# The odd mixer's heads: which engine makes the low parts of the weight units

## The reference, cut to what matters

```
proj = h @ w_in                               # q, k, v, o (16 heads x 128 each), gates ig, fg
q, k = silu(conv4(q)), silu(conv4(k))         # depthwise, causal, 4 taps
# per head, over the 512 tokens, with stabilised exponential gates:
sw  = (q k^T) * weights(gates)                # causal
num = sw @ v ; den = sum(sw)
h   = num / max(|den|, exp(-m)) ; h = rmsnorm(h) * head_norm
y   = sigmoid(o) * h ; x = x + y @ w_out
```

## Time and profile before

| | |
|---|---|
| time of the profiled execution | 4507.37 us |
| its span, first to last instruction | 4505.9 us |
| mean granted TensorE clock | 0.979 of full |
| TensorE busy with matmuls | 4281.0 us, 95% |
| VectorE busy | 2660.6 us, 59% |
| ScalarE busy | 2114.7 us, 47% |
| GpSimd busy | 1237.0 us, 27% |
| low parts on VectorE (L163) | 585 instructions |
| low parts on GpSimd (L170) | 109 instructions |
| the 15 bodies of the odd mixer | 2236.53 to 2710.15 us |

### The profile page before, as it was taken

How to read it: one execution, slowest core, us unless ns; L and a number is a source line. 1 busy time by engine, 2 the same in 40 slices (tenths; PEclk the granted TensorE clock), 3 DMA queues, 4 the chain that set the end, 5 groups by cost and what they waited for, 6 DMA issues and landing times. The chain is left out here.

```text
span 4505.9 us, 61663 instructions
## 1 busy us (share of the span) xinstructions
PE 4281.0 (95%) x19295; PEld 3459.1 (77%) x19295; DVE 2660.6 (59%) x5626; ACT 2114.7 (47%) x4073; POOL 1237.0 (27%) x1571
## 2 busy tenths in 40 slices
PE   7999899999999999999798988999999999999997
PEld 5665687888888888887577776787888888888885
DVE  3546589777764444444566663687877754444444
ACT  2755343677763333333345452433787743333324
POOL 0210245777750000000100000345888720000000
PEclk9999999999999999999899999999999999999998
DMA  2111233555566656542122222334555575656531
GB/s 100 62 47 40 82 116 125 208 180 200 179 256 211 206 172 209 182 159 83 50 75 77 74 77 70 112 117 163 186 203 182 200 261 192 209 170 207 187 121 56
DMA packets 178192, 653.90 MB, mean 145 GB/s; under 512 B 17200, under 2 KB 17328, under 8 KB 172928
## 3 DMA queue, kind: packets, MB, share of 16 engines
q1 hardware_dynamic: 100944, 371.41, 25.2%
q0 software_dynamic: 40240, 213.69, 13.4%
q10 hardware_dynamic: 36864, 67.13, 4.0%
HBM read 507.42 MB, written 144.74 MB: 145 GB/s over the span
## 5 line engine op out<-in xcount | busy, mean ns | idle before, releaser
L184 PE MATMUL ps<-h_hi,w_hi 128*128 128x512 f32 x4296 | 1698.6, 395 | 153.2 <-PEq L280 52.0
L184 PE MATMUL ps<-h_hi,w_lo 128*128 128x512 f32 x4296 | 1683.8, 392 | 0.0
L184 PE MATMUL ps<-h_lo,w_hi 128*128 128x512 f32 x4296 | 1683.7, 392 | 0.0
L163 DVE TENSOR_TENSOR w_lo<-w_raw,w_hi 128x1024 fp32r<-128x1024 f32 x585 | 718.5, 1228 | 1047.7 <-ACT w_hi L157 1042.8
L157 ACT ACTIVATE w_hi<-w_raw 128x1024 fp32r<-128x1024 f32 x694 | 735.8, 1060 | 903.7 <-PE ps L184 730.3
L184 PEld LDWEIGHTS ps<-h_hi,w_hi 128*128 128x128 f32 x4296 | 813.1, 189 | 334.8 <-issue 91.4
L184 PEld LDWEIGHTS ps<-h_hi,w_lo 128*128 128x128 f32 x4296 | 812.5, 189 | 173.4
L184 PEld LDWEIGHTS ps<-h_lo,w_hi 128*128 128x128 f32 x4296 | 814.0, 189 | 160.9 <-issue 0.2
L1481 POOL TENSOR_SCALAR second_hot<-iota,token_keys 128x128 fp32r<-128x128 f32 x1024 | 721.7, 718 | 0.0
L1519 ACT ACTIVATE first_scaled<-first_hot,token_keys 128x128 fp32r<-128x128 f32 x1792 | 542.3, 390 | 0.5 <-DVE first_scaled L1451 0.4
L170 POOL TENSOR_TENSOR w_lo<-w_raw,w_hi 128x1024 fp32r<-128x1024 f32 x109 | 282.9, 2597 | 716.9 <-ACT w_hi L157 716.9
(11 more groups left out here) (308 smaller groups left out, 3516.0 us busy)
## 6 DMA issues: line engine op xcount, KB each, us to landing
w_raw<-in_u SPq DMA_DIRECT2D x256, 512.0 KB, 3.6
w_raw<-in_v SPq DMA_DIRECT2D x256, 512.0 KB, 3.6
gates<-gate_group POOLq DMA_DIRECT2D x36, 2048.0 KB, 8.0
acts<-gelu ACTq DMA_DIRECT2D x256, 256.0 KB, 2.2
gate_block<-gates POOLq DMA_DIRECT2D x32, 2048.0 KB, 18.2
gelu_block<-acts POOLq DMA_DIRECT2D x30, 2048.0 KB, 11.9
w_raw<-in_od_in SPq DMA_DIRECT2D x65, 512.0 KB, 3.5
w_raw<-in_ev_in SPq DMA_DIRECT2D x33, 512.0 KB, 3.5
```

The source lines that it names most:

```text
L163: self.nc.vector.tensor_tensor(self.wl[:, slot % SPL, :], self.raw[:, slot, :], self.wh[:, slot % SPL, :].bitcast(F32), ALU.subtract).then ...
L184: ins = self.nc.tensor.matmul(out, a[:, s, w], b[:, k, :], start=first and j == 0 and m == 0, stop=last and j == n - 1 and m == 2)
```

## The change

Five edits, all in `OddMixer`:

1. GpSimd makes its fifth low part (unit 0 of head 1) behind `rsel` and the transfer of the rows to memory, and no longer ahead of them.
2. For each head n = 1 to 15 it makes, behind the issue of the row's transfer, the low parts of units 1, 2, 3 and of the next unit 0: 60 instructions.
3. VectorE no longer makes these 60. The rest of its order is the same.
4. In head 0, ScalarE makes the high part of unit 2 of the head ahead of the silu of k instead of behind it.
5. VectorE's wait for GpSimd's fifth low part ahead of the bodies is gone; behind the bodies it waits for GpSimd's last one before it makes the output units' low parts.

```diff
-        for n in range(5):
+        for n in range(4):
             p.split_lo_pool(pool, self.u0 + n + 1, (self.u0 + n + 1) % RAW)
         pool.wait_ge(self.cleared.sem, self.cleared.at(1))
         pool.wait_ge(self.gin.sem, self.gin.at(3))
         g.tensor_scalar(self.rsel[:, :], self.negG[:, :], p.ident[0:HEADS, 0:1], None, ALU.mult
                         ).then_inc(self.se.sem, 1)
         pool.dma_start(self.held, self.negG[:, :]).then_inc(self.kept.sem, 16)
+        p.split_lo_pool(pool, self.u0 + 5, (self.u0 + 5) % RAW)
         pool.wait_ge(self.kept.sem, self.kept.at(16))
         for n in range(1, HEADS):
             if n > 1:
                 pool.wait_ge(self.ag.sem, self.ag.at(4 * n))
             pool.dma_start(self.row[:, :], self.held[n:n + 1, :].to_broadcast([P, T])).then_inc(self.bc.sem, 16)
+            for j in range(4):
+                p.split_lo_pool(pool, self.h0 + 4 * n + j + 1, (self.h0 + j + 1) % RAW)
@@ scalar
         a.activation(r["ln"], r["ab"], ACT.Ln).then_inc(self.gact.sem, 1)
+        split(0, 1)
         silu(0, 0)
-        split(0, 1)
         split(0, 2)
@@ vector
-        dve.wait_ge(p.sig("w_lo_ready").sem, h0 + 5)
         def body(n, half, i):
             link.enter(i, self.STEP)
-            lo(n, 0)
             conv(n, 0)
-            lo(n, 1)
             normed(n)
             conv(n, 1)
-            lo(n, 2)
             taken_v(n)
             gate(n)
-            lo(n, 3)
@@
+        dve.wait_ge(p.sig("w_lo_ready").sem, o0 + 1)
         ahead(0)
```

More of the change, by code:

```diff
@@ L2027, in vector @@
         negG, cols, qk, tmp = self.negG, self.cols, self.qk, self.tmp
-        def lo(n, j):
-            p.split_lo(dve, n * 4 + h0 + j + 1, (h0 + j + 1) % RAW)
         def conv(n, j):
```

## The result

Four runs of the changed kernel took 4458.38 us (median; 4457.17 to 4461.97) against 4508.48 (4507.08 to 4509.66): ratio 0.989, 95% interval 0.9873 to 0.9907. The forecast was 4464, the range 4455 to 4482. The profiled execution took 4457.17, its span is 4455.6 us, 50.3 shorter than before.

What follows compares the result with a forecast made beforehand. TensorE, busy 95%, was taken to bound the kernel, waiting 3.3 us a body for VectorE's low part of unit 3 behind conv of q. 4507.4 - 28.5 (bodies) - 3.9 (head 0) - 11.3 (clock) = 4463.7 us; range 4455 to 4482.

Steps and rivals of the forecast that it cites:

- The steady body: Each of the 15 mixer bodies falls from 30.7 to 28.8 us, 28.5 us in all, between 18 and 33.
- D: Rival: GpSimd's low parts, length L, stretch; TensorE starts unit 3 at 10.0 + 2L; slower, 4532 us; chance 0.04.
- the signs by which I would have called the prediction wrong: Bodies above 29.5 us at full clock, TensorE waiting for VectorE's last copy ahead of `output`, or low clocks staying.
- VectorE's loop: VectorE's work per body, including being held by GpSimd: 28.7 us, about as long as TensorE's.
- TensorE's chain through unit 2: In a body: unit 0's product, conv of k, silu, high part, GpSimd's low part, unit 2's product; 28.6 us.
- the worked-out 28.6: TensorE's loop per body: unit 3 starts at 14.9 instead of 17.03, so 30.7 becomes 28.6 us.
- What the engines do to each other: VectorE and GpSimd instructions reading SBUF alone exclude each other for their whole length, the later waiting: the lock.
- Rival B: VectorE's loop decides, through meetings with GpSimd at the masks and late conv of k: body 29.5, 4474 us; chance 0.18.
- Head 0: `rsel` no longer waits behind GpSimd's fifth low part, starting at 2218.9 instead of 2222.84: 3.9 us gained.
- The clock: Of 13.0 us lost to 1.2 GHz stretches in the bodies, 11.3 return, between 0 and 13; 1.7 may stay.
- Rival A: The clock doesn't come back in the bodies, low stretches stay as many: 4475 us; chance 0.12.
- C: Rival: the bodies get no relief, TensorE's wait returning at unit 2; only head 0 pays: 4503 us; chance 0.02.

Runs made afterwards that it cites:

- order: The kernel before with one line moved: VectorE makes unit 3's low part ahead of conv of q, nothing goes to GpSimd; 4445.12 us, ratio 0.9859.
- stretch: The changed kernel with a GpSimd memset of about 1.8 us between high and low part of units 2 and 3 in each body; 4510.87 us, ratio 1.0009.
- bodies: The changed kernel with head 0 as before (edits 1 and 4 taken back); 4462.79 us, ratio 0.9899.
- head0: The kernel before with edits 1 and 4 alone, all low parts of the bodies staying on VectorE; 4504.14 us, ratio 0.9993.
- order_head0: The kernel before with unit 3's low part moved ahead of conv of q on VectorE, plus edits 1 and 4; 4442.46 us, ratio 0.985.

## Why the prediction was right, and where it was off

**What bounded the kernel.** Right, and the reading carried the whole case: TensorE waited for one low part that stood behind conv of q. `order` shows it directly.

**The steady body.** I took 28.8 and so 28.5 us; measured 28.45, so 15 x 2.26 = 33.9. Some marks came true: the low parts take 2.39 to 2.51, conv of q's first step 1.67, `args` of head 0 start at 2222.34, and `stretch` shows both low parts in series as D's rule of 10.0 + 2L had it, in its slope (unit 3 starts 3.4 later for 2 x 1.8 us; at L = 2.4 it starts at 14.25 and not at 14.8). Others did not. TensorE waits for a low part once in a body and not twice: 0.25 at unit 2, not 1.0, and nothing at unit 3, not 0.2. And one of the signs by which I would have called the prediction wrong is there: TensorE waits for VectorE's last copy ahead of `output`, in all of the 14 bodies looked at. The forecast of the time is right, its account of what ends a body is not: that is VectorE's loop, not TensorE's chain through unit 2. That the number came out near in spite of it is in part luck, since the two loops lie within some 0.3 us. Of the 5.4 us by which the term was too small, 3.0 are the step from the worked-out 28.6 to 28.8, an allowance for the lock, and 2.3 the worked-out 28.6 itself against 28.45; the rest is rounding. At unit 2 TensorE waits less because `output` itself starts some 0.35 later: the same lateness, split in two.

**What the engines do to each other.** Right in the meetings, and they were the bound: all four came out as worked through (norm 0.74, conv's first step 1.67, args 3.38, masks 3.10). One row was misread: VectorE's product from 743.74 ends at 748.11, which is not the end of GpSimd's instruction (745.96) but about its own 2.29 behind that; the rule drawn from it holds. VectorE's loop was put at 28.7, "about as long as TensorE's"; it is the longer one, by some 0.3. Rival B was thus true in its place and wrong in its price (29.5). What the prediction lacks is the other side: it counted relief of VectorE as what "goes", and never asked what the same order change would give without GpSimd. The 4.9 us taken from VectorE came back as 6.1 of being held (20.3 - 4.9 + 6.1 = 21.5), and 1.2 us a body of TensorE's time with it (28.45 against 27.22).

**Head 0.** 3.9 predicted, 3.6 measured, but as a sum of two, so that the near match is luck: edit 1, the `rsel` part, gives 6.6 (52.09 to 45.50), and edit 4, costed at 0 "within 1", costs 3.0. Of the 6.6, 3.7 is the row's earlier start (40.0 to 36.3 us from the mixer's start), which is what I had at 3.9; the other 2.9 is clock, since row and scores ran at half speed before, behind a wait of 4.25 for `rsel`, and at full speed without edit 4. Edit 4's effect on VectorE was the 0 that I gave; the step that failed is that I costed it by VectorE alone and not by where TensorE's slow stretches then fall.

**The clock.** 11.3 predicted, 12.7 measured (13.0 of loss before, 0.3 left over a flat 15 x 28.45, and that at clock 1.00). The 1.7 that I expected to stay in the first body did not. Rival A is out; rivals C and D did not happen.

The sum was 43.7; measured 50.2 by the two profiled executions (4507.37 to 4457.17): 5.4 from the body, 1.4 from the clock, -0.3 from head 0.

## What to carry to other kernels

When the bounding engine waits for an engine that is itself half idle, look first at what stands ahead of the awaited instruction in that engine's order; moving one line gave 64 us here, where moving 60 instructions to a second engine gave 44 alone (`bodies`) and 50 with the head-0 edits. GpSimd as a helper isn't free for VectorE: a subtraction of 2.4 us there held up the VectorE instructions under it that had two SBUF inputs (masks, the norm's step), and `args` and conv's first step, which have one. And an edit that moves TensorE's idle time also moves its stretches at half speed: here one under a product that nobody awaited cost nothing, and one under the row and the scores cost 3.0 us.

## What the runs showed of the hardware that I had not expected

- The length of an idle piece of TensorE alone didn't tell whether the clock fell behind it. In head 0 it fell behind 2.03 us (0.66 over the next 5 us, in all six traces with ScalarE's old order) and behind 2.83 us (0.54 over 7.5 us, in the changed kernel, `head0` and `order_head0`), not behind 1.71; in the bodies before, with 3.3 us of idle time in each, it stayed at 1.00 in 8 of 15. What decides it no run here shows.
- A held instruction shows up as a long busy one: VectorE's busy time rose by 1.2 us a body while it was given 4.9 us less to do.
- GpSimd's memsets hold `args` (3.23 in place of 1.27) and leave `TENSOR_TENSOR` with two SBUF inputs alone (0.90 for four masks, 3.10 under subtractions). Conv of q's first step, a `TENSOR_SCALAR` like `args`, they held hardly at all (0.63 in place of 0.55); why is open.
